# Expert value rows on TensorE: four experts of 32 tokens in four column strips, where two of 64 tokens stood in two

## The reference, cut to what matters

```python
u = jnp.take(u_tab, eb, axis=0)
act = jax.nn.gelu(jnp.einsum('cd,ced->ce', xb, u, preferred_element_type=jnp.float32),
                  approximate=False)
v = jnp.take(v_tab, eb, axis=0)
out = jnp.einsum('ce,ced->cd', (gb * act).astype(v.dtype), v, preferred_element_type=jnp.float32)
```

## Time and profile before

| | |
|---|---|
| median of the runs | 2028.65 us (2020.08 to 2028.9) |
| span of the profiled execution | 2029.6 us; no time of its own is given beside the span |
| gathers of u and v in it | from 376 us to 2015 us |
| busy: PE, DVE, ACT, POOL | 72%, 59%, 19%, 53% |
| granted TensorE clock, mean | 0.83 of full speed |
| data moved | 706 MB, of which 612 MB in the queue of the gathers and the cache copies |

### The profile page before, as it was taken

The page is one execution under the profiler, slowest core; times in us unless marked ns, Lnnn a source line. Parts: engine busy times, 40 slices in busy tenths (PEclk is TensorE's granted clock), DMA queues, the critical chain, the costliest instruction groups (busy, mean ns, idle before and its releaser), DMA issues.

```text
span 2029.6 us, 18882 instructions
## 1 busy us (share of the span) xinstructions
PE 1467.7 (72%) x5470; PEld 670.5 (33%) x5470; DVE 1202.8 (59%) x3335; ACT 380.8 (19%) x923; POOL 1067.7 (53%) x1082
## 2 busy tenths in 40 slices
PE   8999998756886687768996555555555666676657
PEld 5444443443443333322442222222222233221111
DVE  1034352585577567667666776677676777687541
ACT  2113441222222222111111111211111212111101
POOL 3020000264575566766566666666666666666674
PEclk9999999976897888778997877777777777776778
DMA  9999998697999799999999989999999999998997
GB/s 329 359 310 365 362 318 304 199 323 260 389 388 362 274 375 343 396 397 375 396 364 403 376 332 344 342 365 361 368 352 368 347 352 357 354 361 332 369 369 284
DMA packets 226136, 706.43 MB, mean 348 GB/s; under 512 B 21153, under 2 KB 46657, under 8 KB 226009
## 3 DMA queue, kind: packets, MB, share of 16 engines
q0 software_dynamic: 166912, 612.40, 80.5%
q1 hardware_dynamic: 59120, 92.82, 13.2%
HBM read 700.65 MB, written 72.61 MB: 381 GB/s over the span
## 4 chain that ended last, share of the span: by engine, by line
PE 26%; DVE 23%; issue 19%; DMA 11%; POOL 9%; another core or an unknown queue 8%; ACT 1%; SPq 1%; DVEq 0%; POOLq 0%; ACTq 0%
PE bank L1059 7%; PE bank L947 4%; DVE XS L1463 4%; POOL WR L660 4%; DVE GT L1463 3%; DMA arena<-in_peer_u_dram,e_all 3%; PE bank L1175 3%; POOL XS L660 2%; DMA WR<-in_peer_v_dram,arena 2%; DVE arena L1463 2%; PE bank L1076 2%; PE bank L1196 2%; PE bank L1154 2%; DMA WR<-in_w_in_dram 2%
## 5 line engine op out<-in xcount | busy, mean ns | idle before, releaser
L1059 PE MATMUL bank<-WR,arena 128*64 128x512 f32 x1728 | 536.1, 724 | 189.8 <-issue 82.1
L660 POOL DMA_INDIRECT WR<-in_peer_v_dram,arena x432 | 427.0, 988 | 301.0 <-issue 145.4
L660 POOL DMA_INDIRECT XS<-in_peer_u_dram,e_all x258 | 269.2, 1043 | 225.7 <-DVE XS L1463 77.4
L1059 PEld LDWEIGHTS bank<-WR,arena 128*64 128x64 f32 x1728 | 146.8, 163 | 520.2 <-issue 470.2
L1463 DVE SCALAR_TENSOR_TENSOR XS<-XS,bank 128x1024 f32<-128x1024 f32 x144 | 171.2, 1218 | 41.3 <-DMA XS<-in_peer_u_dram,e_all 38.8
L1463 DVE SCALAR_TENSOR_TENSOR GT<-GT,bank 128x1024 f32<-128x1024 f32 x126 | 150.0, 1218 | 59.8 <-DMA GT<-in_peer_u_dram,e_all 45.3
L1463 DVE SCALAR_TENSOR_TENSOR XS<-XS,GT 128x1024 f32<-128x1024 f32 x114 | 137.4, 1225 | 80.1 <-DMA XS<-in_peer_u_dram,e_all 65.6
L660 POOL DMA_INDIRECT GT<-in_peer_u_dram,e_all x126 | 123.1, 977 | 52.3 <-issue 33.9
L660 POOL DMA_INDIRECT arena<-in_peer_u_dram,e_all x128 | 127.4, 995 | 42.1 <-issue 37.8
L754 ACT ACTIVATE XS<-bank 128x256 f32<-128x256 f32 (+1 forms) x90 | 36.2, 405 | 469.1 <-remote 267.7
L1076 PE MATMUL bank<-WR,XS 128*128 128x512 f32 x256 | 116.0, 607 | 0.4 <-ACT arena L754 0.4
(11 more groups left out here) (234 smaller groups left out, 2122.9 us busy)
## 6 DMA issues: line engine op xcount, KB each, us to landing
out_dram<-in_cache_a_k_dram POOLq DMA_DIRECT2D x8, 4064.0 KB, 54.6
out_dram<-in_cache_a_v_dram POOLq DMA_DIRECT2D x8, 4064.0 KB, 55.4
WR<-in_w_in_dram SPq DMA_DIRECT2D x8, 2048.0 KB, 25.7
GT<-in_w_peer_q_dram SPq DMA_DIRECT2D x14, 1024.0 KB
WR<-in_w_out_dram SPq DMA_DIRECT2D x6, 2048.0 KB
WR<-in_peer_v_dram,arena POOLq DMA_INDIRECT x432
WR<-in_w_branch_a_dram SPq DMA_DIRECT2D x6, 1024.0 KB, 7.6
WR<-in_w_branch_b_dram SPq DMA_DIRECT2D x6, 1024.0 KB, 9.7
```

The source lines that it names most:

```text
L660: nc.gpsimd.indirect_dma_start(dst, None, table, bass.IndirectOffsetOnAxis(ap=idx, axis=0))\
L1059: last = nc.tensor.matmul(b[c][R * j:R * j + R, :], diag[p // QUAD % 4][:, s % 4, :], V[V_AT[s]][:, c * CHUNK:(c + 1) * CHUNK], start=Fals ...
```

## The change

`G` becomes 4 and so `R` 32. The v ring loses its middle form: it keeps 8 buffers up to quad 80 and has 12 from there.

```diff
-G = 2
+G = 4
 R = P // G
...
-WIDER_U, WIDER_V, WIDEST_V = 44 * QUAD, 56 * QUAD, 80 * QUAD
+WIDER_U, WIDEST_V = 44 * QUAD, 80 * QUAD
...
 def v_buffer(s):
 
-    if s < WIDER_V:
-        return s % 8
-    return (s - WIDER_V) % 10 if s < WIDEST_V else (s - WIDEST_V + 10) % 12
+    return s % 8 if s < WIDEST_V else (s - WIDEST_V) % 12
```

## The result

The changed kernel takes 2040.3 us (median of 20 runs, 2026.74 to 2058.07), the kernel before 2028.78 us beside it (20 runs, 2015.93 to 2043.05): ratio 1.0057, 95% interval 1.0033 to 1.0081. It is slower by about 0.6%, which the interval sets clear of no change, where 0.2% faster was forecast.

What follows compares the result with a forecast made beforehand. The prediction took DMA as the bound by a little, POOL next. Its terms, -6 + 3 + 0 - 3 + 2 + 1 = -3 us against 2029.6 us, gave 2026 us by the median, stated as 2025 us; range 1999 to 2046 us.

Steps and rivals of the forecast that it cites:

- the terms cancel: Main case for the whole kernel: gains and costs nearly balance, giving 2015 to 2036 us; chance 0.46.
- ACT late: Rival: ACT's copies arrive slowly and DVE waits 21 us and more for them, about 2042 us; chance 0.05.
- The bound: DMA bounds the kernel by a little, POOL is next; any gain must come from 95 us of DMA idle time.
- PE's v products: Expert products on PE: a quad takes what a pair took, some 310 us of PE go, buffers come free earlier; -6 us.
- The ring of 8: Shorter v ring in quads 56 to 79: longer waits against PE being less late, between -9 and +27; +3 us.
- short ring decides: Rival: PE stays late in quads 57 to 77, so +15 to +27 us stand; about 2044 us; chance 0.13.
- The ring of 12: v ring after quad 80: 6.3 us of waits may go or grow, -3 to +3; taken as 0.
- the end: End of the program: the first v set of quad 128 waits for all of the sample's second quad; +1 us.
- DVE waits for PE: Attention part, up to 900 us: freer PE gives scores and u buffers earlier; -3 us, between 0 and -16.
- ACT's copies: Regroupings on ACT: 16 copies take 3.5 us, mostly covered, while DVE's diagonals get shorter; +2 us, between -5 and +15.
- The clock: Rival: idler PE gets a lower clock, v products run at half clock and PE stays late; about 2040 us; chance 0.06.
- The stalls of all engines: "Remote" stalls the change doesn't reach; if they move with instruction count, ACT's 768 added ones count too; no size given.

Runs made afterwards that it cites:

- r_four: The changed kernel with 4 copies of 64 x 8 in each regrouping, leaving pairings wrong, a second time on the slower chip: ratio 1.0008 to the kernel before.
- e6_four: The changed kernel with the old 4 copies of 64 x 8 in each regrouping, so rows and weights are wrongly paired: ratio 1.0006 to the kernel before.
- e7_whole: e1_ring's kernel, with PE waiting for all four buffers of a quad and handing them back once a quad: ratio 1.0069 to the kernel before.
- e10_landed: e1_ring's kernel, with PE waiting for all four buffers of a quad but still handing back after each pair: ratio 0.9995 to the kernel before.
- e1_ring: The kernel before with only its v ring changed (8 buffers up to quad 80, then 12): ratio 0.999.
- r_after: The changed kernel itself, measured again on a faster chip: ratio 1.0033 to the kernel before.
- e5_turns: The kernel before with each regrouping cut into 16 copies of 64 x 2, rows changing from copy to copy: ratio 1.0051.
- r_after2: The changed kernel itself once more, on another of the faster chips: ratio 1.0047 to the kernel before.
- e8_twice: The changed kernel with every v product of the prompt issued twice, with halved stationary matrices: ratio 1.0106 to the kernel before.
- e12_index4: The changed kernel with 4 copies for indices (experts of other pairings gathered) and 16 for weights: ratio 1.0021 to the kernel before.
- e13_weight4: The changed kernel with 16 copies for indices and 4 for weights (rows weighted in a wrong pairing): ratio 1.0025 to the kernel before.

## Why the prediction was wrong

It forecast that the terms cancel at -3 us; they came out at about +12 us at the slower chip's level and +6 to +9 us on the others. The forecast case, that the terms cancel, was wrong in direction and in size; the time lies in the range only because the slow cases stretched it to 2046 us. Of the 15 us between forecast and result on the first chip, some 7 lie in the terms without the copies (-5 us forecast, +2 us in r_four) and some 8 in the copies (+2 us forecast, 10 us measured). "ACT late" gave 2042 us, near the result, but by another path: it wanted over 20 us of DVE waiting for ACT, and there were 12.3 us.

- *The bound* was read rightly, and drawn on too little. DMA was the bound, on the faster chips fully so after 1050 us (share 1.02). 310 us of PE's time were forecast to go; 186 us of the v products' went (627 to 440), since the clock fell. (The shares of the 29 us are 13.6 and 15.4 us, where the prediction has 13 and 16.)
- *PE's v products.* A quad in 1.92 us came true at the full clock. The waits before 1165 us fell by 16 us and 13 of 20 went, the long ones staying, as the step said. **The -6 us for it did not come:** with 4 copies, the ring and everything else changed, the kernel is at +1 us and +2 us (e6_four and r_four, 0.0006 x 1900 and 0.0008 x 2023; the first interval goes from -2 to +4 us). The step counted the waits that go, and took nothing for a hand-back that now comes once a quad. On two strips that hand-back alone costs 14 us (e7_whole less e10_landed, 0.0074 x 1902); four strips win back some 12 us (e7_whole less e6_four) and no more. That the hand-back is what eats the -6 us follows from these differences; no run has four strips with a hand-back for each pair.
- *The ring of 8*, +3 us: nothing measurable (e1_ring -2 us, between -9 and +5, so +3 is not excluded). The case "short ring decides" is out, also by the 10.0 us of waits there. *The ring of 12* (0) and *the end* (+1 us) had no run of their own; POOL's waits for PE after 1465 us are 6.9 us and were 6.3.
- *DVE waits for PE*, -3 us: POOL's waits for DVE's u products fell from 53.9 to 42.7 us in the first stretch, but no time shows for it.
- **ACT's copies, +2 us, is the term that was mis-sized.** The duration was right (3.48 us), the diagonals got 17 us shorter as forecast (53.8 to 36.7 us), and the cover held at the place where it was read: DVE waited for weights twice in the whole run (8.6 us, once each at 1722 and 2002 us). Measured, the 16 copies cost 5 us (r_after less e6_four, 0.0027 x 1902, on two chips of one level) to 10 us (0.0057 less 0.0008, x 2030), and 10 us in e5_turns. The intervals of these pairs still touch; that three measurements of the changed kernel (1.0033 to 1.0057) lie above both with 4 copies (1.0006 and 1.0008), and e5_turns clear above 1, carries the finding. Two assumptions failed. "Index copies have two steps of time" holds for all heads but the first, where 2.6 us are uncovered and the first v gather goes out some 2 to 4 us late. And the step asked only who waits for the copies, not what stands behind them on ACT: two evacuations at 920 us, which make POOL wait some 3 us longer. By the count of gathers the second place is worth about 5 us on the faster chips, of the 5 to 8 us that the copies cost there (r_after and r_after2 less e6_four), and the late start nothing that lasts in the changed kernel; on the slower chip the two make some 8 of 10 us. Why the start lasts on one chip and not on the others is open.
- *The clock* went under 0.7 after 1165 us with v quads of 3.5 us (median), one of the signs named for that rival. It was not the cause: e6_four has that clock and no loss, e8_twice the old clock and three times the loss of r_after. The Trainium skill (TensorE: Matmul & The Clock Gate, HAM oscillation) says that the clock comes down where PE waits between bursts of matmuls. This trace agrees (mean granted clock 0.828 before, 0.760 after); here it cost only time that PE had over.
- *The stalls of all engines* are there again: 101 us of "remote" waits of POOL for v buffers in the three stretches, and 77 us before. Whether they grow with the copies on ACT stays open. On the faster chips no kernel has them from 1050 to 1850 us, not even e8_twice with 23620 instructions, so the loss there is not theirs. On the slower chip they are, in that window, 45.3 to 64.0 us in the three profiles with 4 copies (before 60.8, e1_ring 64.0, r_four 45.3) and 65.2 to 71.2 us in the five with 16 in every regrouping; e12_index4 has 35.6 and e13_weight4 63.8. That is one profiled run of each.

The signs "L1057 some 320 us", "waits for PE under 25 us" and "DVE hardly waits for L779" were missed (440, 31.3, and 12.3 us); ACT at 540 us and the DMA shares were met.

## What to carry to other kernels

When a helper's instructions multiply, look not only at who waits for its result but at what stands behind it on its engine, and at its first use, which has no earlier step to hide in. A cheaper engine gains nothing where transfers are full: count its relief only in the stretch where they are not. And a larger unit of work comes with a later hand-back of its first buffers; four strips here were just fast enough to make up for that.

## What the runs showed of the hardware

- *Small copies on ACT cost by their order.* 16 copies of 64 x 2 took 1.95 us with the same rows four times in a row and 3.40 us with rows changing each time; 16 of 32 x 4 took 3.48 us. On DVE 16 of 32 x 4 took 3.15 us. Whether the rows or the distance in the source decide was not tried.
- *Four strips run side by side in either order of the loops:* at the full clock 1.92 us for 16 MATMULs with the strips in turn (3.64 us at half clock), 1.94 us with two matmuls of one strip in succession.
- *Chips 6 to 7% apart.* Before takes 2022 to 2031 us on one and 1900 to 1904 us on three others. On these three the DMA share from 1050 to 1850 us is 1.02 to 1.03 at 407 GB/s, on the one 0.94 to 0.96 at 356 to 362 GB/s. In the changed kernel's first profile POOL waited 68.5 us for "remote" in that stretch, in r_after not at all. Why the engines of the slower chip stand together remains open.
